# Column slabs as one 512-column product: both activation parts into two halves of a bank

## Chip, cores, metric

One core of a Trainium2 chip (trn2). The metric is the device time of one launch in microseconds; every run is timed alone.

## What is computed

The kernel computes a float32 forward pass over 256 tokens of width 1024: two layers (a gated recurrence with pooling, then a convolution block; each followed by cross-attention and a convolutional FFN), and a third layer with banded attention and a mixture of 32 experts. The part that the change touches most is the FFN, twice, with `D_FF = 3072` and `CONV_F = 3`:

```python
def conv_ffn(x, norm, w_up, dw_w, dw_b, w_down):
    h = rms_norm(x, norm) @ w_up
    g = causal_dwconv(h[..., :D_FF], dw_w, dw_b)
    u = h[..., D_FF:]
    return (jax.nn.gelu(g) * u) @ w_down
```

The other products that change are `k = m @ wk` and `q = rms_norm(x) @ wq` of the cross-attention, the pointwise product `h = rms_norm(x) @ w1 + b1; h = glu(h)` of the convolution block, and the first columns and the gates of the third layer's in-projection `x @ w_in`.

## The kernel before

**Layout.** Activations lie turned: 128 channels on the partitions, 256 tokens along the free side (`T = 256`), eight chunks for the width (`KC = 8`). Weights come from memory as *slabs* of 128 x 1024 floats through a ring of 12 places (`raw`), issued by SyncE in the order of `PHASES`. A *column slab* holds the weights of 128 output columns for all eight chunks; `col_slab` multiplies it and leaves 128 x 256 results in one of four PSUM banks `pw` (512 floats wide, used to the half). A *row slab* holds 128 input rows for all 1024 outputs and adds into the four banks `acc`.

**Split products.** Products must keep float32 accuracy, so each factor is held as a sum of a high and a low part in a shorter format (fp32r). ScalarE writes the high part of a slab (`wh`, line 733), VectorE (line 1259, every second slab) or POOL (line 1142, the others) subtracts to get the low part (`wl`). Both have four places (`SPLIT`), filled three slabs ahead (`AHEAD`). The activations are split likewise into `ah`, `al` (and `mh`, `ml` for the memory tokens). `tile3` (lines 2064 to 2066) makes the product of one chunk with three matmuls, high x high, low weight x high, high weight x low, all into the same 256 columns:

```python
pe.matmul(dst, wh[...], hi, start=start, stop=False)
pe.matmul(dst, wl[...], hi, start=False, stop=False)
pe.matmul(dst, wh[...], lo, start=False, stop=stop)
```

**Norms.** A product starts on the unnormed activation; the reciprocal root mean square of each token (`rstd_b`) is multiplied in when VectorE takes the result out of its bank. The first three slabs of a phase (`LEAD`, function `lead`) run ahead of that and stay with the three 256-column products; the taking out ("drain") of a slab is `col_out` (lines 1327, 1329), `slab_out` (1393, first keys), `gate_out` (1749, fills) and `gate` and `up` in the FFN (1570, 1589).

**The FFN loop** (`glu`, J = 24 steps, four of them in the body of a hardware loop). Step j on TensorE: gate slab j, up slab j, row slab j - 2. On VectorE: drain of the gate slab into `gpad` (with two zero columns ahead), three taps of the convolution (1576, then 1579 twice) into `cf`, drain of the up slab into `uf`, and `hid = cf * uf` (1592) once ScalarE has put the GELU on `cf`; its splits stand between. ScalarE and POOL then split `hid` for the row slab. A bank is free for TensorE when its drain has raised `empty_v` (`bank_free`); two steps use the four banks in turn.

**Order.** Every engine's order is written out by hand, and semaphores count it. `V.fence()` makes VectorE wait for its own last instruction. In the third layer's attention 16 gate columns ("fills", `FILLS`) run between the score products; all use bank `pw[3]`, so each waits for the drain of the one before (`gate_out`). After the in-projection the expert weights (1 MB per transfer) come through a ring of 18 places, and the last quarter of the run multiplies them as they land.

## Time and profile before

| | |
|---|---|
| median of 3 runs | 1674.98 us (1674.19 to 1675.51) |
| span of the profiled execution | 1674.9 us |
| TensorE busy (matmul) | 1628.1 us, 97% |
| TensorE weight loads | 1290.0 us, 77% |
| VectorE busy | 830.0 us, 50% |
| ScalarE, POOL busy | 601.2 us, 471.2 us |
| memory read, written | 394.02 MB, 1.05 MB |

The times are whole runs; the span is one profiled execution, from its first to its last instruction, and the profile gives no other time for it; it lies 0.1 us under the median. Busy time of TensorE is that of overlapping matmuls with modelled ends, so what a matmul costs is read from the distance between starts. Shares are means over stages with different limits; the stages are looked at one by one.

### The profile page before, as it was taken

The page shows a single profiled execution, that of the slowest core. Times are in us where ns is not written, and L with a number is a line of the kernel's source. Part 1 is how long each engine was busy: PE and PEld are TensorE (multiplying, and loading weights), DVE is VectorE, ACT ScalarE, POOL GpSimd, SP SyncE. Part 2 cuts the span into 40 slices and gives each one's busy share as a digit, 9 for nine tenths or more (in the row PEclk, how much of TensorE's full clock was granted, in tenths as well). Part 3 has the DMA queues.
Part 4 walks back from the last instruction along what each step waited for, and adds up shares of the span by engine and source line. Part 5 has one row for each costly group of instructions (what it writes and reads, how often), then busy time and mean ns, then how long its engine had stood idle before and what let it go on. Part 6 is the DMA issues. An engine that isn't in the chain of part 4 may idle for free.

```text
span 1674.9 us, 28612 instructions
## 1 busy us (share of the span) xinstructions
PE 1628.1 (97%) x11476; PEld 1290.0 (77%) x11476; DVE 830.0 (50%) x1320; ACT 601.2 (36%) x1019; POOL 471.2 (28%) x257
## 2 busy tenths in 40 slices
PE   7999999999999999999999999999999999999996
PEld 6898998999999699899999998888944444444332
DVE  2665457888875174688887433768711010110102
ACT  2371454444453264444345333656311111111101
POOL 1332424555543142355555443222200000000000
PEclk9999999999999999999999999999999999999999
DMA  7464634555559453455552665262899999999995
GB/s 296 151 218 157 211 114 139 184 180 176 182 183 262 165 165 116 136 188 176 179 185 90 209 217 176 89 229 87 319 394 421 421 422 421 421 422 420 421 421 220
DMA packets 86055, 401.21 MB, mean 240 GB/s; under 512 B 9536, under 2 KB 14272, under 8 KB 61248
## 3 DMA queue, kind: packets, MB, share of 16 engines
q1 hardware_dynamic: 84944, 395.81, 64.5%
q10 hardware_dynamic: 1008, 3.96, 0.6%
q8 instruction: 74, 1.21, 0.3%
q14 instruction: 29, 0.24, 0.0%
HBM read 394.02 MB, written 1.05 MB: 236 GB/s over the span
## 4 chain that ended last, share of the span: by engine, by line
PE 42%; issue 30%; DVE 22%; ACT 4%; POOL 1%; DVEq 1%; DMA 0%; ACTq 0%; SPq 0%; POOLq 0%
DVE wl L1259 6%; DVE cf L1576 5%; PE pw L2064 5%; PE pw L2066 5%; PE pw L2065 5%; PE pw L2377 4%; DVE hid L1592 4%; ACT wh L733 3%; DVE cf L1579 3%; PE acc L2070 2%; PE acc L2064 2%; PE acc L2065 2%; PE acc L2066 2%; PE acc L2236 2%; DVE gpad L1570 1%
## 5 line engine op out<-in xcount | busy, mean ns | idle before, releaser
L1142 POOL TENSOR_TENSOR wl<-raw,wh 128x1024 fp32r<-128x1024 f32 x157 | 387.4, 2468 | 569.4 <-ACT wh L733 565.7
L733 ACT ACTIVATE wh<-raw 128x1024 fp32r<-128x1024 f32 x314 | 325.1, 1051 | 230.8 <-PE pw L2066 104.9
L2064 PE MATMUL pw<-ah,wh 128*128 128x256 f32 x1272 | 364.5, 287 | 5.0 <-POOL wl L1142 3.4
L2065 PE MATMUL pw<-ah,wl 128*128 128x256 f32 x1272 | 359.8, 283 | 0.0
L2066 PE MATMUL pw<-al,wh 128*128 128x256 f32 x1272 | 359.8, 283 | 0.0
L1259 DVE TENSOR_TENSOR wl<-raw,wh 128x1024 fp32r<-128x1024 f32 x157 | 200.9, 1280 | 117.2 <-ACT wh L733 117.0
L2064 PEld LDWEIGHTS pw<-ah,wh 128*128 128x128 f32 x1272 | 243.7, 192 | 10.4 <-issue 6.3
L2065 PEld LDWEIGHTS pw<-ah,wl 128*128 128x128 f32 x1272 | 243.9, 192 | 0.1
L2066 PEld LDWEIGHTS pw<-al,wh 128*128 128x128 f32 x1272 | 243.8, 192 | 0.0
L2064 PE MATMUL acc<-yh,wh 128*128 128x256 f32 x672 | 194.0, 289 | 2.0 <-POOL yl L1211 1.2
L2065 PE MATMUL acc<-yh,wl 128*128 128x256 f32 x672 | 190.1, 283 | 0.0
L2066 PE MATMUL acc<-yl,wh 128*128 128x256 f32 x672 | 190.0, 283 | 0.0
L1153 POOL TENSOR_TENSOR small<-small 128x2 f32<-128x2 f32 x12 | 12.1, 1005 | 527.9 <-DVE small L1276 523.6
L2064 PEld LDWEIGHTS acc<-yh,wh 128*128 128x128 f32 x672 | 128.6, 191 | 5.7 <-issue 3.1
L2065 PEld LDWEIGHTS acc<-yh,wl 128*128 128x128 f32 x672 | 128.7, 192 | 0.1
L2066 PEld LDWEIGHTS acc<-yl,wh 128*128 128x128 f32 x672 | 128.7, 192 | 0.0
L2015 DVE COPY slot_gate<-pw 64x1 f32<-64x1 f32 x32 | 5.0, 156 | 235.0 <-ACT slots_to_tokens L1088 234.5
L1576 DVE TENSOR_SCALAR cf<-gpad,cols 128x256 f32<-128x256 f32 x48 | 90.2, 1879 | 7.5 <-DVE gpad L1570 6.9
L2377 PE MATMUL pw<-x_gained,raw 128*128 128x256 f32 x320 | 74.0, 393 | 8.3 <-DMA raw<-in_stream 8.3
L886 ACT ACTIVATE cf<-cf 128x256 f32<-128x256 f32 x48 | 20.1, 418 | 164.4 <-DVE cf L1579 164.1
L2656 PE MATMUL pw<-raw,gathered 128*64 128x512 f32 x328 | 77.0, 601 | 1.2 <-DMA raw<-in_experts 0.8
L1211 POOL TENSOR_TENSOR yl<-hid,yh 128x256 fp32r<-128x256 f32 x48 | 50.2, 1045 | 96.9 <-ACT yh L890 96.9
(335 smaller groups left out, 2569.2 us busy)
## 6 DMA issues: line engine op xcount, KB each, us to landing
raw<-in_stream SPq DMA_DIRECT2D x358, 512.0 KB, 3.5
raw<-in_experts SPq DMA_DIRECT2D x65, 1024.0 KB, 24.3
ring_w<-in_experts SPq DMA_DIRECT2D x40, 1024.0 KB, 24.3
ring_y<-in_experts SPq DMA_DIRECT2D x30, 1024.0 KB, 23.0
early_e<-in_experts SPq DMA_DIRECT2D x22, 1024.0 KB, 20.8
ring_q<-in_experts SPq DMA_DIRECT2D x11, 1024.0 KB, 21.9
ring_k<-in_experts SPq DMA_DIRECT2D x11, 1024.0 KB, 22.7
ring_a<-in_experts SPq DMA_DIRECT2D x11, 1024.0 KB, 23.4
```

Source lines behind the costliest of these rows:

```text
L733: A.done(act.activation(wh[:, s.base % SPLIT, :], raw[:, slot_of(s.base), :], ACT.Copy), w_hi)
L1142: G.done(pool.tensor_tensor(wl[:, s.base % SPLIT, :], raw[:, slot_of(s.base), :], wh[:, s.base % SPLIT, :].bitcast(F32), ALU.subtract), w_ ...
L1211: G.done(pool.tensor_tensor(yl[:, j % 4, :], hid[:, j % 2, :], yh[:, j % 4, :].bitcast(F32), ALU.subtract), S("ffn_hid_lo"))
L1259: V.done(dve.tensor_tensor(wl[:, s.base % SPLIT, :], raw[:, slot_of(s.base), :], wh[:, s.base % SPLIT, :].bitcast(F32), ALU.subtract), w_lo_v)
L1576: V.done(dve.tensor_scalar(cf[:, j % 2, :], gpad[:, j % 2, 2:T + 2], w, col(f"f_dw_b{l}", j, 4, i), ALU.mult, ALU.add))
L1579: V.done(dve.scalar_tensor_tensor(cf[:, j % 2, :], gpad[:, j % 2, 2 - k:T + 2 - k], w, cf[:, j % 2, :], ALU.mult, ALU.add), S("ffn_conv") ...
L1592: V.done(dve.tensor_tensor(hid[:, j % 2, :], cf[:, j % 2, :], uf[:, j % 2, :], ALU.mult), S("ffn_hidden"))
L2064: pe.matmul(dst, wh[:, s.base % SPLIT, w], hi, start=start, stop=False, **kw)
L2065: pe.matmul(dst, wl[:, s.base % SPLIT, w], hi, start=False, stop=False, **kw)
L2066: return pe.matmul(dst, wh[:, s.base % SPLIT, w], lo, start=False, stop=stop, **kw)
L2377: last = pe.matmul(pw[u % 4][:, 0:T], raw[:, slot_of(n), k * P:k * P + P], ax[:, k, :], start=(k == 0), stop=(k == KC - 1))
L2656: ins = pe.matmul(pw[bank + h][rows, :], stationary(e), expert_pair(s.base - S0["moe"])[:, e, 512 * h:512 * h + 512], start=first, stop=la ...
```

## The change

The high and the low part of an activation become one tile `a_pair` (and `m_pair`) with two halves. `tile2` replaces `tile3` in column slabs that are not of the first three: one matmul streams both halves past `wh` (512 columns, the whole bank: left half high x high, right half high weight x low), and one of 256 columns adds low weight x high to the left half. VectorE now has to add the two halves: `halves_added` with one reduction where nothing is multiplied (the keys), `halves_scaled` with two multiplications by `rstd_b` (the low half into a spare tile, the high half in place) and then an addition. In the FFN the sum stays in the bank, the convolution reads it there, and so does the product `hid`; `gpad` and `uf` go. A gate bank is then free when the last tap is done (`ffn_conv`), an up bank when `hid` is done (`ffn_hidden`), and `bank_free` waits for these.

```diff
+            def halves_added(bank, dst, sem):
+                V.done(dve.tensor_reduce(dst, bank[:, 0:2 * T].rearrange("p (h t) -> p t h", h=2), AX.X, ALU.add), sem)
+            def halves_scaled(bank, low, scale=None):
+                high = bank[:, 0:T]
+                V.fence()
+                for dst, src in ((low, bank[:, T:2 * T]), (high, high)):
+                    if scale is None:
+                        V.done(dve.tensor_tensor(dst, src, rstd_b[:], ALU.mult))
+                    else:
+                        V.done(dve.scalar_tensor_tensor(dst, src, scale, rstd_b[:], ALU.mult, ALU.mult))
+                V.fence()
+                return high
...
             def col_out(name, n, dst, scale=None, by=None, slab=None):
                 if by is None:
-                    ins = dve.tensor_copy(dst, b)
-                elif scale is None:
+                    halves_added(pw[u % 4], dst, empty_v)
+                    return
+                if name != "abin" and n >= LEAD:
+                    low = t[1][:] if name == "win" else low_t[:]
+                    ins = dve.tensor_tensor(dst, halves_scaled(pw[u % 4], low, scale), low, ALU.add)
+                    V.done(ins, empty_v)
+                    return
...
-                    V.done(dve.tensor_tensor(gpad[:, j % 2, 2:T + 2], pw[(USE0[name] + 2 * j) % 4][:, 0:T],
-                                             rstd_b[:], ALU.mult), empty_v)
+                    bank = pw[(USE0[name] + 2 * j) % 4]
+                    g = bank[:, 0:T]
+                    if 2 * j >= LEAD:
+                        halves_scaled(bank, low_t[:])
+                        V.done(dve.tensor_tensor(g, g, low_t[:], ALU.add))
+                    else:
+                        V.done(dve.tensor_tensor(g, g, rstd_b[:], ALU.mult))
...
-                            V.done(dve.tensor_scalar(cf[:, j % 2, :], gpad[:, j % 2, 2:T + 2], w,
-                                                     col(f"f_dw_b{l}", j, 4, i), ALU.mult, ALU.add))
+                            V.done(dve.tensor_scalar(cf[:, j % 2, :], g, w, col(f"f_dw_b{l}", j, 4, i),
+                                                     ALU.mult, ALU.add))
...
-                    V.done(dve.tensor_tensor(uf[:, j % 2, :], pw[u % 4][:, 0:T], rstd_b[:], ALU.mult), empty_v)
+                    up_b = pw[u % 4][:, 0:T]
+                    if 2 * j + 1 >= LEAD:
+                        halves_scaled(pw[u % 4], low_t[:])
+                        V.done(dve.tensor_tensor(up_b, up_b, low_t[:], ALU.add))
...
+                    V.done(dve.tensor_tensor(hid[:, j % 2, :], up_b, cf[:, j % 2, :], ALU.mult), S("ffn_hidden"))
...
-                    V.done(dve.tensor_tensor(gt[:, n - 46, :], pw[3][:, 0:T], rstd_b[:], ALU.mult), S("gate_out"))
+                    V.done(dve.tensor_tensor(gt[:, n - 46, :], halves_scaled(pw[3], t[1][:]), t[1][:], ALU.add), S("gate_out"))
...
+            def tile2(bank, s, n, pair, start, stop):
+                w = slice(n * P, n * P + P)
+                pe.matmul(bank[:, 0:2 * T], wh[:, s.base % SPLIT, w], pair, start=start, stop=False,
+                          skip_group_check=True)
+                return pe.matmul(bank[:, 0:T], wl[:, s.base % SPLIT, w], pair[:, 0, :], start=False, stop=stop,
+                                 skip_group_check=True)
...
-                    pe.wait_ge(empty_v, (jj + -2).of(lambda n: v0 + 2 * n + (1 if kind == "g" else 2)))
+                    pe.wait_ge(S("ffn_conv" if kind == "g" else "ffn_hidden"), (jj + -1).of(lambda n: n + ffn0(name)))
```

TensorE, the first two chunks of the first key slab (`pw` is the bank, `mh` and `ml` the parts of the memory tokens). Before:

```order
L2064 MATMUL pw<-mh,wh 128x256
L2065 MATMUL pw<-mh,wl 128x256
L2066 MATMUL pw<-ml,wh 128x256
L2064 MATMUL pw<-mh,wh 128x256
L2065 MATMUL pw<-mh,wl 128x256
L2066 MATMUL pw<-ml,wh 128x256
```

and with the change:

```order
L2100 MATMUL pw<-m_pair,wh 128x512
L2102 MATMUL pw<-m_pair,wl 128x256
L2100 MATMUL pw<-m_pair,wh 128x512
L2102 MATMUL pw<-m_pair,wl 128x256
```

Six matmuls for two chunks become four.

VectorE, the fourth step of the first FFN loop, ahead of the hardware loop (`wl` is a split of a later slab, `cf` the convolution, `pw` a bank). Before:

```order
L1570 TENSOR_TENSOR gpad<-pw,rstd_b 128x256
L1576 TENSOR_SCALAR cf<-gpad,cols 128x256
L1579 SCALAR_TENSOR_TENSOR cf<-gpad,cols,cf 128x256 x2
L1589 TENSOR_TENSOR uf<-pw,rstd_b 128x256
L1592 TENSOR_TENSOR hid<-cf,uf 128x256
L1259 TENSOR_TENSOR wl<-raw,wh 128x1024
```

and with the change:

```order
L1329 TENSOR_TENSOR low_t<-pw,rstd_b 128x256
L1329 TENSOR_TENSOR pw<-pw,rstd_b 128x256
L1596 TENSOR_TENSOR pw<-pw,low_t 128x256
L1603 TENSOR_SCALAR cf<-pw,cols 128x256
L1606 SCALAR_TENSOR_TENSOR cf<-pw,cols,cf 128x255
L1606 SCALAR_TENSOR_TENSOR cf<-pw,cols,cf 128x254
L1329 TENSOR_TENSOR low_t<-pw,rstd_b 128x256
L1329 TENSOR_TENSOR pw<-pw,rstd_b 128x256
L1619 TENSOR_TENSOR pw<-pw,low_t 128x256
L1624 TENSOR_TENSOR hid<-pw,cf 128x256
L1259 TENSOR_TENSOR wl<-raw,wh 128x1024
```

The two drains are now three instructions each, all on the bank, and the taps and `hid` read the bank; the split keeps its place at the end.

## Rows read from the trace of the kernel before

**Rows 1.** The page, busy time of each engine, share of the span and instructions.
```profile
PE 1628.1 (97%) x11476; PEld 1290.0 (77%) x11476; DVE 830.0 (50%) x1320; ACT 601.2 (36%) x1019; POOL 471.2 (28%) x257
```

**Rows 2.** The page, lines on the chain of work that ended last, shares of the span.
```profile
DVE wl L1259 6%; DVE cf L1576 5%; PE pw L2064 5%; PE pw L2066 5%; PE pw L2065 5%; PE pw L2377 4%; DVE hid L1592 4%; ACT wh L733 3%; DVE cf L1579 3%; PE acc L2070 2%; PE acc L2064 2%; PE acc L2065 2%; PE acc L2066 2%; PE acc L2236 2%; DVE gpad L1570 1%
```

**Rows 3.** Table by stretch: us; busy of PE, PEld, DVE, ACT, POOL; PEclk, DMA share, GB/s.
```profile
275.45:465.34 189.89, 189.28 (x1561) 188.04 (x1561) 156.11 (x168) 81.01 (x113) 103.86 (x55) 1.00 0.55 180
1041.00:1122.00 81.00, 78.39 (x663) 67.61 (x660) 55.17 (x96) 48.35 (x109) 18.51 (x8) 1.00 0.38 132
1230.00:1640.00 410.00, 402.23 (x2028) 167.53 (x2028) 38.99 (x88) 56.64 (x102) 0.00 (x0) 1.00 1.01 419
```

**Rows 4.** TensorE in time, FFN loop: start, length, engine, line, operation (x count) [idle].
```profile
400.05 0.28 PE L2066 MATMUL pw<-al,wh 128*128 128x256 f32 x1
...
400.17 0.28 PE L2064 MATMUL pw<-ah,wh 128*128 128x256 f32 x1
```

**Rows 5.** TensorE in time, value slabs of the in-projection.
```profile
1010.04 0.39 PE L2200 MATMUL pw<-wh,al 128*128 128x512 f32 x1
1010.26 0.39 PE L2198 MATMUL pw<-wh,ah 128*128 128x512 f32 x1
```

**Rows 6.** VectorE in time, two steps of the FFN loop.
```profile
400.02 0.42 DVE L1589 TENSOR_TENSOR uf<-pw,rstd_b 128x256 f32<-128x256 f32 x1
400.57 2.44 DVE L1592 TENSOR_TENSOR hid<-cf,uf 128x256 f32<-128x256 f32 x1
404.44 1.23 DVE L1259 TENSOR_TENSOR wl<-raw,wh 128x1024 fp32r<-128x1024 f32 x1 [1.44 <-ACT wh L733]
...
406.32 1.75 DVE L1576 TENSOR_SCALAR cf<-gpad,cols 128x256 f32<-128x256 f32 x1 [0.19 <-DVE gpad L1570]
408.22 1.11 DVE L1579 SCALAR_TENSOR_TENSOR cf<-gpad,cols,cf 128x256 f32<-128x256 f32 x2
...
412.64 2.46 DVE L1576 TENSOR_SCALAR cf<-gpad,cols 128x256 f32<-128x256 f32 x1 [0.19 <-DVE gpad L1570]
...
417.53 0.42 DVE L1589 TENSOR_TENSOR uf<-pw,rstd_b 128x256 f32<-128x256 f32 x1
```

**Rows 7.** POOL in time, the same stretch.
```profile
400.33 2.40 POOL L1142 TENSOR_TENSOR wl<-raw,wh 128x1024 fp32r<-128x1024 f32 x1 [2.89 <-ACT wh L733]
...
412.55 2.40 POOL L1142 TENSOR_TENSOR wl<-raw,wh 128x1024 fp32r<-128x1024 f32 x1
```

**Rows 8.** Instructions on tile gpad: ns min/median/max, first and last start.
```profile
L1570 DVE TENSOR_TENSOR gpad<-pw,rstd_b x48: 424/425/427, 264.0 to 890.6; 128x256 f32<-128x256 f32 x48
```

**Rows 9.** VectorE in time, queries of layer 0.
```profile
196.07 1.09 DVE L1329 SCALAR_TENSOR_TENSOR q_t<-pw,rstd_b 128x256 f32<-128x256 f32 x3
```

**Rows 10.** VectorE by line and shape: busy us, mean ns | idle before, releaser.
```profile
L1576 DVE TENSOR_SCALAR cf<-gpad,cols 128x256 f32<-128x256 f32 x48 | 90.2, 1879 | 7.5 <-DVE gpad L1570 6.9
...
L1779 DVE TENSOR_REDUCE small<-sc 128x2 f32<-128x514 f32 x8 | 5.5, 688 | 0.3
...
L1447 DVE TENSOR_SCALAR z<-pw,cols 128x256 f32<-128x256 f32 x4 | 2.2, 540 | 3.0 <-PE pw L2070 3.0
```

**Rows 11.** Waits of TensorE, start of FFN 0: us in total, times, longest.
```profile
PE pw L2064 <- POOL wl L1142: 1.7, 1, 1.7
```

**Rows 12.** VectorE in time, start of FFN 0.
```profile
267.46 0.85 DVE L1576 TENSOR_SCALAR cf<-gpad,cols 128x256 f32<-128x256 f32 x1
```

**Rows 13.** VectorE in time, queries of layer 0, slabs 5 and 7.
```profile
204.33 0.42 DVE L1329 SCALAR_TENSOR_TENSOR q_t<-pw,rstd_b 128x256 f32<-128x256 f32 x1 [1.34 <-PE pw L2066]
...
212.54 0.42 DVE L1329 SCALAR_TENSOR_TENSOR q_t<-pw,rstd_b 128x256 f32<-128x256 f32 x1 [1.43 <-PE pw L2066]
```

**Rows 14.** VectorE in time, pointwise product of the convolution block.
```profile
504.70 2.20 DVE L1645 TENSOR_SCALAR t<-t 128x256 f32<-128x256 f32 x1 [0.99 <-ACT t L919]
```

**Rows 15.** TensorE in time, second fill product in attention.
```profile
1048.89 0.35 PE L2064 MATMUL pw<-ah,wh 128*128 128x256 f32 x1 [0.61 <-DVE gt L1749]
```

**Rows 16.** The chain in order of time, first in-projection on unsplit data.
```profile
42.01 44.90 PE pw L2377 x208
```

More of the change, by code:

```diff
@@ L361, in program @@
         cv = sb("cv", "arena", 34, [P, KC, T])
-        gpad = sb("gpad", "arena", 24, [P, 2, T + 2])
         cf = sb("cf", "arena", 27, [P, 2, T])
-        uf = sb("uf", "arena", 29, [P, 2, T])
         hid = sb("hid", "arena", 31, [P, 2, T])
+        low_t = sb("low_t", "arena", 33, [P, T])
         q2 = sb("q2", "arena", 0, [P, 20, T])
@@ L1588, in up @@
                     V.fence()
-                    V.done(dve.tensor_tensor(uf[:, j % 2, :], pw[u % 4][:, 0:T], rstd_b[:], ALU.mult), empty_v)
+                    up_b = pw[u % 4][:, 0:T]
+                    if 2 * j + 1 >= LEAD:
+                        halves_scaled(pw[u % 4], low_t[:])
+                        V.done(dve.tensor_tensor(up_b, up_b, low_t[:], ALU.add))
+                    else:
+                        V.done(dve.tensor_tensor(up_b, up_b, rstd_b[:], ALU.mult))
                     V.fence()
                     dve.wait_ge(S("ffn_act"), (jj + 1).of(lambda n: n + ffn0(name)))
-                    V.done(dve.tensor_tensor(hid[:, j % 2, :], cf[:, j % 2, :], uf[:, j % 2, :], ALU.mult),
-                           S("ffn_hidden"))
-                V.fence()
-                V.done(dve.memset(gpad[:, :, 0:2], 0.0))
+                    V.done(dve.tensor_tensor(hid[:, j % 2, :], up_b, cf[:, j % 2, :], ALU.mult), S("ffn_hidden"))
                 trips, rest = glu_steps(J)
@@ L2095, in drain, with col_slab @@
             def drain(u):
-                for who, sem in (("v", empty_v), ("a", empty_a)):
+                for who, sem in emptier.items():
                     if u and emptied(u - 1, who):
                         pe.wait_ge(sem, emptied(u - 1, who))
-            def col_slab(s, u, hi, lo, wait_n=None, first_ready=None):
+            def col_slab(s, u, pair, wait_n=None, first_ready=None):
                 wait_split(pe, s)
@@ L2108, in col_slab, with col_phase @@
                         first_ready(k)
-                    last = tile3(pw[u % 4][:, 0:T], s, k, hi[:, k, :], lo[:, k, :], k == 0, k == KC - 1)
+                    last = tile2(pw[u % 4], s, k, pair[:, :, k, :], k == 0, k == KC - 1)
                 last.then_inc(slab_done, 1)
-            def col_phase(name, n, hi, lo, ready=None, hook=None, straight=None, s_off=0, u_off=0):
+            def col_phase(name, n, pair, ready=None, hook=None, straight=None, s_off=0, u_off=0):
                 s0, u0 = S0[name] + s_off, USE0[name] + u_off
@@ L2119, in col_phase @@
                         wait_emptied(pe, u0 + k - 4)
-                    col_slab(At(s0 + k), u0 + k, hi, lo, None, ready if k == 0 else None)
+                    col_slab(At(s0 + k), u0 + k, pair, None, ready if k == 0 else None)
                     if hook:
@@ L2125, in col_phase @@
                         for j in range(straight, straight + 4):
-                            col_slab(At(s0 + j, 4, i), u0 + j, hi, lo, i * 4 + (v0 + j - 3))
+                            col_slab(At(s0 + j, 4, i), u0 + j, pair, i * 4 + (v0 + j - 3))
             def lead(phase, name, pair):
@@ L2449, in final_spread @@
                     norm_spread("final")
-            col_phase("win", 32 - LEAD, ah, al, spread_at("mix"), final_spread, 5, LEAD, LEAD)
+            col_phase("win", 32 - LEAD, a_pair, spread_at("mix"), final_spread, 5, LEAD, LEAD)
             for b in range(3):
@@ L2478, in fill @@
                         for k in range(KC):
-                            last = tile3(pw[3][:, 0:T], s, k, ah[:, k, :], al[:, k, :], k == 0, k == KC - 1)
+                            last = tile2(pw[3], s, k, a_pair[:, :, k, :], k == 0, k == KC - 1)
                         last.then_inc(slab_done, 1)
```

43 lines of the change are left out of this document (22 added, 21 removed).

## Prediction

> **What bounds the kernel now.** I read the page's busy shares first [rows 1]: TensorE is busy in 97% of the span. That share is an average, so the chain of waits comes next [rows 2]: three of the costliest lines on it are VectorE's, the split (line 1259), the first convolution op of the FFN (line 1576) and the last product there (line 1592). So somewhere VectorE sets the pace under a TensorE that looks full. The table by stretch [rows 3] says where to look: the first FFN loop takes 189.89 us with TensorE busy all the time; the attention stage with its fill products has 2.6 us of idle TensorE in 81; the expert stage moves 419 GB/s with the DMA engines full, so it ends a fixed time after it can start, and what is won ahead of it is taken over whole.
>
> TensorE's price is read from starts, since the shown durations overlap. Products of 256 columns follow each other every 0.12 us [rows 4], those of 512 columns every 0.227 [rows 5]. At 2.4 GHz (granted clock 1.00 in all three stretches) the columns alone are 0.107 and 0.213, so both carry the same 0.013. The loop has 65 slabs of 24 products: 65 x 2.88 = 187.2 of its 189.89 us. The other 2.7 us are VectorE's: from one `uf` at 400.02 to the one two steps on at 417.53 are 17.51 us [rows 6], where six slabs want 17.28. In these two steps `hid` takes 2.44 and `cf` 1.75 and 2.46; each ends where a POOL subtraction ends (400.33 + 2.40, 412.55 + 2.40) [rows 7]. VectorE ops with both tensor inputs in SBUF wait for POOL there; `gpad`, with an input in PSUM, took 424 to 427 ns in all 48 cases [rows 8].
>
> **The product.** 175 slabs change: 8 (first keys), 2 x 5 (queries), 2 x 45 (FFN), 13 + 8 (pointwise, second keys), 46 (in-projection with its fills). Three products per chunk at 3 x 0.12 become one of 512 and one of 256: 0.227 + 0.12 = 0.347. A slab falls from 2.88 to 8 x 0.347 = 2.776, by 0.104; 18.2 us if TensorE set the pace everywhere. The two extremes: nothing saved (the third part's 256 columns cost in the long product what they cost alone: 0), or the short product also loses its fixed part, its weights loaded behind a long one (0.335 a chunk, 0.2 a slab). I take the rows as they stand.
>
> **VectorE's new work.** A drain was one op; now it is low half times scale, high half times scale in place, and the add. Prices: back to back 0.34 (three `q_t` in 1.09) [rows 9]; behind a fence 0.55 (`uf` to `hid` 0.55) to 0.61 (0.42 and a gap of 0.19) [rows 6]. So a drain costs some 0.9 more. Writing to PSUM stands in no row: below, 0.42 as for SBUF; above, twice that. I take 0.42, the figure for the same op with the same input, and keep the other as a rival.
>
> **The FFN loops.** A gate becomes 0.34 + 0.55 + 0.61, then the convolution from the bank: 0.54 by the nearest op with two column operands and a PSUM input [rows 10] and 0.15 of fence, two taps 1.19 with theirs (1.11 for the pair) [rows 6]; 3.4 together. The up half is 0.34 + 0.55 + 0.55 + 0.46 = 1.9. Two steps with three splits at 1.26: 2 x 5.3 + 3.8 = 14.3 us, since `cf` and `hid` now have only one input in SBUF and should not wait for POOL. The VectorE page of the Trainium skill (VectorE: DVE Perf Modes, "Rules for kernel authors") advises to copy a product to SBUF first if many ops read it, as this kernel does now. By that advice the old convolution would be the better one; here it meets POOL in most steps and takes 1.88 us in the mean [rows 10], so I follow the rows.
> TensorE then needs 4 x 2.776 + 2 x 2.88 = 16.86 for two steps, more than 14.3, and becomes the bound: 42 column slabs and 23 row slabs are 182.8 us against 189.89, so -7.1. The bank is now freed by the last tap and not the first drain, and the other by `hid`; each is used again two steps later, some 14 us after its slab, so that wait is covered by the loop itself. If the cover went, it would show as TensorE waiting at a gate slab. At the start of a loop TensorE stands 1.7 us for a POOL split [rows 11], at the end of a chain through gate and up of steps 0 and 1. There the up of step 1 gains 0.9 and a convolution op loses 0.3 (0.85 to 0.54) [rows 12]; +0.6, and the gain of the first slabs vanishes in that stall. Net -6.4 a loop, **-12.9** for both.
>
> **First keys.** Eight drains become a reduction over both halves: 0.69 for some 512 elements [rows 10] instead of 0.42. VectorE hands over the first values late already, so the slabs' 0.8 is not seen: **+0.5**.
> **Queries, twice.** The drain of slab 5 stands ahead of the first row maxima (204.33) and that of slab 7 ahead of the second (212.54) [rows 13]; TensorE waits for the exponentials behind them. Two longer drains less the shorter slabs: +1.2 each, **+2.4**.
> **Pointwise and second keys.** 21 slabs give -2.2. In a pair VectorE had 5.76 us with a wait of 0.99 for tanh and an op held for 2.20 [rows 14]; now 1.25 (split) + 2 x 1.4 + 0.99 + about 0.8 + 0.5 = 6.3 against 5.55. It falls behind 0.7 a pair, 4.6 in all; the split for three slabs ahead leaves about 3.3 of that unseen. The later key slabs catch up. **-0.9**.
> **In-projection.** 30 slabs in a row, VectorE needs 4.1 us of 5.55 for two: **-3.1**.
> **Fills.** 16 products share one bank, so the next one waits for the drain. Where it stands right behind it, as at 1048.89 (0.61 idle) [rows 15], the longer drain shows in full. I count four such at 0.75 and twelve at 0.2, which the score products cover mostly: 5.4, less 16 x 0.104: **+3.7**. Its ends: -1.7 (all covered) and +12 (all seen).
>
> SP, ACT and POOL get no instruction more or less. Sum: -12.9 + 0.5 + 2.4 - 0.9 - 3.1 + 3.7 = -10.3. The profiled span is 1674.9, the median of the runs 1674.98, so one correction serves both: **1664.5 us**. With each stage's ends it lies between 1656 and 1672.
>
> **Rivals.**
> A. *The product is not cheaper.* The 512-column product costs 0.24, as two of 256. For it: products on unsplit data of 256 columns and two passes follow every 216 ns (44.90 us for 208) [rows 16], which is the columns and nothing fixed. Against it: [rows 5], which are with split data. Then two FFN steps take 17.28, each loop wins 2.7 - 0.6 = 2.1, and the costs elsewhere stay (keys 0.5, queries 3.0 without the shorter slabs, fills 5.4): 1674.9 - 4.2 + 8.9 = 1679.6. The TensorE page of the Trainium skill (TensorE: Matmul & The Clock Gate, "Back-to-back issue gap") states columns over the clock plus 2.5 ns; by it a slab would win under 0.02 us and this rival would hold. The starts shown here carry 13 ns and disagree. It decides as soon as a slab wins less than about 0.03, where the other costs eat the gain.
> B. *VectorE stays the bound.* Writes to PSUM (eight in two steps) cost 0.85 instead of 0.42: 14.3 + 3.4 = 17.7 in two steps, 0.84 over TensorE's, 21 pairs: +17.6, and some 3 more in the other drains: 1685. For it: no row shows such a write. Against: reading PSUM cost nothing extra. It decides above 17.35 in two steps.
> C. *The short product gains too.* 0.335 a chunk, 2.68 a slab: two steps 16.5, each loop -10.5, the in-projection -6, the fills +2.2, the rest as above: 1652. For it: the products of [rows 16], which have no fixed part.
> D. *Attention pays more.* The fills cost +10 (for 3.7) and the queries +5 (for 2.4): 1673. For it: exactly these drains stand on a chain with exponentials; against: TensorE idles only 2.6 us there [rows 3], so most drains have cover.
> That the change does not do what it says is excluded: the matmul count of a slab falls from 24 to 16.
>
> **Numbers.** Forecast 0.60, A 0.08, B 0.06, C 0.11, D 0.15. Two runs of this kernel differ by 1.3 us at most; 0.2% is 3.3 us, about what can be told from no change. Faster (below 1671.6): forecast 0.60, C 0.11 and a third of D, 0.76. Same: the rest of D, 0.10. Slower: A and B, 0.14. The range goes from just under C to the middle between D and A: 1649 to 1678. It leaves out A, B and the far side of C.
>
> **What would show it.** Right: starts 0.227 and 0.12 apart in a column slab; the FFN loop at 183 us with 8.43 per step, `cf` near 0.55 and `hid` near 0.45 in every step; VectorE waiting for TensorE's slabs in it. Wrong: two steps still near 17.5 with VectorE on the chain (B), chunks at 0.36 (A), or TensorE waiting for the fills' drains for more than 10 us (D).

## The result and the profile after

The changed kernel takes 1681.3 us (median of 6, 1680.33 to 1683.36) against 1675.46 for the kernel before (median of 6): a ratio of 1.0038 (95% interval 1.0027 to 1.0048), 5.8 us slower where 10.5 us faster were forecast. In every later run the time stands 1.8 us above the span, so the profiled execution of before belonged to a launch of some 1676.7, 1.2 above its median; the two traces differ by 5.0. The span of a launch and its time, which the prediction set equal, are thus not the same. One of the eleven executions of run 3 below took 2293 us at a mean granted clock of 0.65; its median counts it, its ratio does not.

The page of the changed kernel, busy times and the lines on the chain:

```profile
PE 1614.7 (96%) x10076; PEld 1213.4 (72%) x10076; DVE 849.0 (51%) x1636; ACT 608.2 (36%) x1019; POOL 463.1 (28%) x257
...
PE pw L2100 16%; PE pw L2102 8%; PE acc L2093 4%; PE acc L2094 4%; PE acc L2095 4%; PE pw L2413 4%; PE acc L2107 2%; DVE wl L1259 2%; PE acc L2273 2%; PE pw L2186 1%; PE pw L2235 1%; PE pw L2237 1%; PE pw L2236 1%; PE pw L2187 1%; PE pw L2176 1%
```

TensorE has 1400 products less than in [rows 1] and is 13.4 us less busy, and VectorE's convolution and `hid` have left the chain of [rows 2]. The time won is idle time now. Where, the starts of TensorE's stages tell. In this table, worked out from the traces, the first row is the start of a stage in the kernel before (first product of it, us), the others how much later (+) the same start lies in another kernel; `run1` to `run11` are the experiments below:

```
          q0     wo0    FFN0   pw1    k1     conv   q1     FFN1   win    att    out    experts end
before    182.7  226.1  249.3  465.3  514.5  537.6  618.9  685.0  900.9  1039.7 1121.7 1216.9  1674.9
changed   +0.4   +1.1   +1.1   -3.4   +1.8   +3.2   +3.2   +3.6   -0.8   -2.7   +2.5   +3.8    +5.0
run1      +0.3   +1.0   +1.0   -3.5   +1.7   +2.7   +3.0   +3.4   -0.8   -2.8   +2.5   +2.4    +4.0
run2      -0.2   +0.5   +0.5   -3.8   -4.2   -4.6   -4.6   -4.2   -8.5   -11.8  -5.0   -5.1    -5.7
run3      +0.8   +1.5   +1.5   -2.8   -3.9   -4.3   -4.3   -3.9   -8.3   -10.2  -3.6   -3.7    -2.3
run4      +0.0   +0.7   +0.7   -3.7   +1.5   +2.5   +2.7   +3.2   -1.2   -3.1   -3.1   -3.3    -1.3
run5      +0.5   +1.3   +1.3   -3.2   -3.6   -4.0   -4.0   -3.5   -7.8   -9.9   -9.9   -10.0   -10.8
run6      -0.4   +0.3   +0.3   -5.9   -6.3   -7.0   -7.0   -6.3   -12.4  -14.9  -14.9  -15.0   -15.7
run7      -0.3   -0.3   -0.3   -3.0   -3.5   -3.5   -3.5   -3.5   -6.1   -6.6   -6.7   -6.8    -7.3
run8      +0.6   +1.3   +1.3   +8.7   +13.8  +14.9  +14.8  +15.3  +21.2  +19.7  +26.4  +26.3   +28.5
run9      -0.4   -0.4   -0.4   -6.5   -7.7   -8.4   -8.4   -8.5   -14.6  -16.7  -16.7  -16.9   -14.0
run10     +0.9   +1.6   +1.6   -2.7   +2.4   +3.5   +3.5   +3.9   -0.5   -3.8   +2.9   +4.2    +5.6
run11     -0.4   +0.3   +0.3   -4.0   +1.2   +2.2   +2.2   +2.7   -1.7   -3.6   +1.7   +1.6    +0.9
```

(`q0`, `q1` queries, `wo0` their output product, `pw1` pointwise, `k1` second keys, `conv` the convolution, `win` in-projection, `att` attention with its fills, `out` what follows them, `experts` the first expert product.) The changed kernel wins 4.5 and 4.4 us in the FFNs and 1.9 in the in-projection, and loses 6.6 between `pw1` and `conv`, 5.2 in attention and 2.5 behind it. The table by stretch for the FFN loop, the pointwise slabs with the second keys, and attention (us; busy of PE, PEld, DVE, ACT, POOL; PEclk, DMA share, GB/s), changed kernel:

```profile
275.45:461.90 186.45, 185.18 (x1228) 169.46 (x1228) 134.89 (x255) 85.19 (x115) 101.23 (x56) 1.00 0.56 184
461.90:540.80 78.90, 71.92 (x438) 61.52 (x436) 59.61 (x94) 28.80 (x43) 29.50 (x13) 1.00 0.64 184
1037.00:1124.20 87.20, 78.83 (x545) 60.88 (x545) 68.58 (x128) 48.31 (x109) 19.09 (x8) 1.00 0.33 122
```

and the second of these stretches in the kernel before:

```profile
465.30:537.60 72.30, 72.30 (x603) 70.79 (x602) 46.35 (x69) 30.27 (x43) 29.60 (x13) 1.00 0.80 215
```

Before, TensorE was never idle there; now it is for 7 of 78.9 us. The third row answers to the second of [rows 3]: 8.4 us idle where 2.6 were.

**The price of a chunk.** TensorE in time, changed kernel, FFN loop (the stretch of [rows 4]):

```profile
400.07 0.40 PE L2100 MATMUL pw<-a_pair,wh 128*128 128x512 f32 x1
400.31 0.28 PE L2102 MATMUL pw<-a_pair,wl 128*128 128x256 f32 x1
400.42 0.40 PE L2100 MATMUL pw<-a_pair,wh 128*128 128x512 f32 x1
400.65 0.28 PE L2102 MATMUL pw<-a_pair,wl 128*128 128x256 f32 x1
```

Over the loop the medians from start to start are 236 ns behind a long product and 117 behind a short one: 353 a chunk, 2.824 a slab. A slab wins 0.056 us, not 0.104.

**The FFN loop.** VectorE in time, changed kernel, part of one step (what answers to [rows 6]):

```profile
408.26 0.42 DVE L1329 TENSOR_TENSOR low_t<-pw,rstd_b 128x256 f32<-128x256 f32 x1 [1.80 <-PE pw L2102]
408.60 0.42 DVE L1329 TENSOR_TENSOR pw<-pw,rstd_b 128x256 f32<-128x256 f32 x1
409.06 0.43 DVE L1596 TENSOR_TENSOR pw<-pw,low_t 128x256 f32<-128x256 f32 x1
409.68 0.54 DVE L1603 TENSOR_SCALAR cf<-pw,cols 128x256 f32<-128x256 f32 x1 [0.19 <-DVE pw L1596]
410.37 1.11 DVE L1606 SCALAR_TENSOR_TENSOR cf<-pw,cols,cf 128x255 f32<-128x255 f32 x2
```

The convolution's first op takes 0.54 where it took 1.75 and 2.46, and VectorE waits 1.80 us for TensorE's slab: here TensorE has become the bound, as forecast.

**The pointwise slabs.** VectorE in time, changed kernel, one pair and the start of the next:

```profile
503.41 0.29 DVE L1674 TENSOR_SCALAR t<-t 128x256 f32<-128x256 f32 x1 [0.58 <-ACT t L919]
503.74 0.49 DVE L1676 SCALAR_TENSOR_TENSOR hpad<-t,cols,t 128x256 f32<-128x256 f32 x1
504.36 0.42 DVE L1329 TENSOR_TENSOR low_t<-pw,rstd_b 128x256 f32<-128x256 f32 x1
504.70 0.42 DVE L1329 TENSOR_TENSOR pw<-pw,rstd_b 128x256 f32<-128x256 f32 x1
505.16 0.42 DVE L1345 TENSOR_TENSOR t<-pw,low_t 128x256 f32<-128x256 f32 x1
505.50 3.32 DVE L1259 TENSOR_TENSOR wl<-raw,wh 128x1024 fp32r<-128x1024 f32 x1
508.95 0.42 DVE L1329 TENSOR_TENSOR low_t<-pw,rstd_b 128x256 f32<-128x256 f32 x1
...
512.84 3.33 DVE L1259 TENSOR_TENSOR wl<-raw,wh 128x1024 fp32r<-128x1024 f32 x1
```

and POOL beside it:

```profile
505.35 2.37 POOL L1142 TENSOR_TENSOR wl<-raw,wh 128x1024 fp32r<-128x1024 f32 x1 [4.96 <-ACT wh L733]
512.69 2.39 POOL L1142 TENSOR_TENSOR wl<-raw,wh 128x1024 fp32r<-128x1024 f32 x1 [4.96 <-ACT wh L733]
```

The splits of one pair to the next in the kernel before, and POOL beside them:

```profile
502.03 1.22 DVE L1259 TENSOR_TENSOR wl<-raw,wh 128x1024 fp32r<-128x1024 f32 x1
...
507.79 1.22 DVE L1259 TENSOR_TENSOR wl<-raw,wh 128x1024 fp32r<-128x1024 f32 x1
```

```profile
504.35 2.40 POOL L1142 TENSOR_TENSOR wl<-raw,wh 128x1024 fp32r<-128x1024 f32 x1 [3.36 <-ACT wh L733]
```

There the split is over before POOL starts. With the change the split of 128x1024 takes 3.32 us where it takes 1.23 alone [rows 6]: POOL began its own subtraction 0.15 us earlier, and VectorE's ends 1.1 us after POOL's. This repeats in all six pairs from 483 us on: 7.34 us from split to split, against 5.76 before and the 5.65 that TensorE needs for two slabs. Between 470 and 550 us 8 of VectorE's 12 splits last over 2 us; before, one did. The ops that write in place in the bank take 0.42 each, as those to SBUF.

**The fills.** Waits of TensorE in attention, changed kernel, for the drain of a fill (us in total, times, longest), and the same waits in the kernel before:

```profile
PE pw L2100 <- DVE gt L1778: 6.9, 9, 1.9
```

```profile
PE pw L2064 <- DVE gt L1749: 1.5, 2, 0.9
```

**Behind the last expert** a branch of TensorE's program, which jumps over a path for overfull experts, took 3.55 us in the changed kernel and 0.36 before (duration in ns: least, median, largest; start):

```profile
L2830 PEldq COMPARE_BRANCH  x1: 3552/3552/3552, 1664.2 to 1664.2; - x1
```

```profile
L2794 PEldq COMPARE_BRANCH  x1: 363/363/363, 1661.4 to 1661.4; - x1
```

TensorE stands in it while the squares for the last norm are ready: from the start of the branch to the end are 15.7 us, 13.5 before. In the router, from `out` to `experts`, another 1.3 us are lost: the granted clock was 0.90 over that stretch for 1.00 before, with a fall to 1.2 GHz inside it. Run 1 has the same instructions there, no such fall and no loss (table), and runs 2, 3, 8 and 10 have one in attention instead, where they lose some 6.7 us for 5.2; so this part belongs to the execution and not to the change. The experts took 1.0 us less, and 2.2 + 1.3 - 1.0 is the 2.5.

### The profile page after: what moved, and what is told of

Read it like the earlier page. It is cut to its first block, busy times and chain, and to the rows that moved or that the text cites. A ratio compares the mean times of both kernels' runs of the same rounds, so it can differ in the third digit from the quotient of the medians.

```text
span 1679.9 us, 26261 instructions
## 1 busy us (share of the span) xinstructions
PE 1614.7 (96%) x10076; PEld 1213.4 (72%) x10076; DVE 849.0 (51%) x1636; ACT 608.2 (36%) x1019; POOL 463.1 (28%) x257
## 4 chain that ended last, share of the span: by engine, by line
PE 59%; issue 29%; DVE 9%; ACT 2%; POOL 1%; DMA 0%; DVEq 0%; SPq 0%; POOLq 0%; ACTq 0%
PE pw L2100 16%; PE pw L2102 8%; PE acc L2093 4%; PE acc L2094 4%; PE acc L2095 4%; PE pw L2413 4%; PE acc L2107 2%; DVE wl L1259 2%; PE acc L2273 2%; PE pw L2186 1%; PE pw L2235 1%; PE pw L2237 1%; PE pw L2236 1%; PE pw L2187 1%; PE pw L2176 1%
## 5 line engine op out<-in xcount | busy, mean ns | idle before, releaser
L2100 PE MATMUL pw<-a_pair,wh 128*128 128x512 f32 x1272 | 455.6, 400 | 16.7 <-DVE gt L1778 6.9
L733 ACT ACTIVATE wh<-raw 128x1024 fp32r<-128x1024 f32 x314 | 328.7, 1053 | 247.2 <-PE pw L2102 118.6
L2102 PE MATMUL pw<-a_pair,wl 128*128 128x256 f32 x1272 | 356.9, 281 | 0.0
L2100 PEld LDWEIGHTS pw<-a_pair,wh 128*128 128x128 f32 x1272 | 239.0, 188 | 77.9 <-issue 14.3
L1259 DVE TENSOR_TENSOR wl<-raw,wh 128x1024 fp32r<-128x1024 f32 x157 | 216.8, 1381 | 94.9 <-ACT wh L733 94.7
L2102 PEld LDWEIGHTS pw<-a_pair,wl 128*128 128x128 f32 x1272 | 240.3, 189 | 0.1
L2413 PEld LDWEIGHTS pw<-x_gained,raw 128*128 128x128 f32 x320 | 62.5, 197 | 17.9 <-issue 8.6
L2031 DVE TENSOR_TENSOR expert_out_lo<-pw,expert_out_hi 128x512 fp32r<-128x512 f32 x32 | 20.7, 687 | 108.3 <-ACT expert_out_hi L1077 108.3
L1329 DVE TENSOR_TENSOR low_t<-pw,rstd_b 128x256 f32<-128x256 f32 x103 | 43.8, 425 | 49.5 <-PE pw L2102 38.9
L1211 POOL TENSOR_TENSOR yl<-hid,yh 128x256 fp32r<-128x256 f32 x48 | 44.8, 933 | 77.4 <-ACT yh L890 77.4
```

The costliest lines, as they stand in the source:

```text
L733: A.done(act.activation(wh[:, s.base % SPLIT, :], raw[:, slot_of(s.base), :], ACT.Copy), w_hi)
L1211: G.done(pool.tensor_tensor(yl[:, j % 4, :], hid[:, j % 2, :], yh[:, j % 4, :].bitcast(F32), ALU.subtract), S("ffn_hid_lo"))
L1259: V.done(dve.tensor_tensor(wl[:, s.base % SPLIT, :], raw[:, slot_of(s.base), :], wh[:, s.base % SPLIT, :].bitcast(F32), ALU.subtract), w_lo_v)
L1329: V.done(dve.tensor_tensor(dst, src, rstd_b[:], ALU.mult))
L2100: pe.matmul(bank[:, 0:2 * T], wh[:, s.base % SPLIT, w], pair, start=start, stop=False, skip_group_check=True)
L2102: return pe.matmul(bank[:, 0:T], wl[:, s.base % SPLIT, w], pair[:, 0, :], start=False, stop=stop, skip_group_check=True)
```

## The experiments

Times are medians; the kernel before took 1675.5 to 1675.9 in these comparisons.

**Run 1, layout.** The tiles become `[P, KC, 2, T]`, so that the halves of a chunk lie side by side.

```diff
-        a_pair = sb("a_pair", "ah", 0, [P, 2, KC, T], F32R)
+        a_pair = sb("a_pair", "ah", 0, [P, KC, 2, T], F32R)
```

> Only the layout of the two activation tiles changes: the halves of one chunk lie side by side, so the 512-column product reads one run of 512 floats and not two of 256. Seen in the changed kernel: starts 236 ns after a 512-column product and 117 after a 256-column one, 353 a chunk, where the value slabs show 227 for 512 contiguous columns. Theory A (the jump between the halves costs the 9 ns): 227 + 120 a chunk, a slab falls by 0.05 us, 84 FFN slabs, 27 of the in-projection and 16 fills gain 5 to 6 us, 1675.5 to 1676. Theory B (the 9 ns belong to the alternation of long and short products): 236 and 117 stay, 1681.

1680.91 us, ratio 1.0035 (1.0022 to 1.0049); the medians are 236 and 117 ns again. The jump between the halves costs nothing: theory A falls.

**Run 2, three products in the pointwise slabs.**

```diff
-            col_phase("pw1", 16 - LEAD, a_pair, spread_at("c"), None, 5, LEAD, LEAD)
+            col_phase("pw1", 16 - LEAD, (ah, al), spread_at("c"), None, 5, LEAD, LEAD)
...
-                if name != "abin" and n >= LEAD:
+                if name not in ("abin", "pw1") and n >= LEAD:
```

> The 13 pointwise slabs alone go back to three 256-column products and a drain of one instruction; all else stays changed. Theory: the 6.9 us that the changed kernel loses between the first pointwise slab and the last slab of the second keys come from VectorE's longer drains in the pointwise pairs (7.34 us a pair for 5.76). Then the pair returns to 5.76 and the time to about 1674. Rival: they come from the keys behind, whose drain is a reduction now (0.69 for 0.42): then it stays at 1680 to 1681.

1671.03 us, 0.9974 (0.9965 to 0.9983). From `pw1` to `conv` it now wins 0.8 us where the changed kernel lost 6.6: 7.4, as expected. The time fell by 3 us more than that. The branch is part of it, 0.48 us here; in this trace the in-projection, too, wins 3.3 us for 1.9 (see run 6).

**Run 3, the split one place earlier.** The same instructions; VectorE's split of the pointwise loop moves ahead of the drain of the even slab.

```diff
-                split(At(S0["pw1"] + n + AHEAD))
+                if not 4 <= n <= 15:
+                    split(At(S0["pw1"] + n + AHEAD))
+                elif n % 2 == 0:
+                    split(At(S0["pw1"] + n + 1 + AHEAD))
```

> The change is kept whole; in the pointwise loop VectorE's split stands one place earlier, ahead of the drain of the even slab, so that it can be done before POOL starts its own subtraction. No instruction more or less. Theory H (the hold is the loss: the split takes 3.31 us in each pair since it starts 0.15 us behind POOL's): the split takes 1.2, a pair falls from 7.34 to 5.7, the time to 1674 to 1675. Rival O (VectorE simply has too many instructions in a pair, as the prediction's 6.3 us had it): the pair stays at 6.3 or more and the time at 1677 or above.

1674.37 us, 0.9985 (0.9976 to 0.9995). VectorE in time, run 3:

```profile
499.20 1.23 DVE L1259 TENSOR_TENSOR wl<-raw,wh 128x1024 fp32r<-128x1024 f32 x1
500.56 0.42 DVE L1329 TENSOR_TENSOR low_t<-pw,rstd_b 128x256 f32<-128x256 f32 x1
...
504.66 1.22 DVE L1259 TENSOR_TENSOR wl<-raw,wh 128x1024 fp32r<-128x1024 f32 x1
```

and POOL:

```profile
500.65 2.40 POOL L1142 TENSOR_TENSOR wl<-raw,wh 128x1024 fp32r<-128x1024 f32 x1 [3.24 <-ACT wh L733]
```

The split ends before POOL starts, the pair takes 5.46 us with all six drain instructions in it, and the stretch from `pw1` to `conv` wins 1.5 us. So it is not the number of instructions (rival O) but the hold: the same work in another order is 8 us shorter there.

**Run 4, three products in the fills** (line 2515 back to `tile3`, `gate_out` back to one multiplication by `rstd_b`).

> The 16 fills alone go back to three products and a drain of one instruction. From the last value slabs to the last fill the changed kernel loses 5.3 us against before. Theory (the longer drain of the one bank that all fills share is seen in full where the next fill waits): 5 to 5.5 us less, 1676. Rival (the loss is elsewhere in attention, in the row maxima and exponentials that stand behind the drains only by chance): less than 2 us, 1679.5 to 1681.

1675.13 us, 0.9997 (0.9987 to 1.0006). From `att` to `out` nothing is lost (-3.1 at both ends), for 5.2 before: the waits for the drain are 1.5 us in 2 again. The run puts back products and drain together, but the three products of a fill take longer than the two, so it is the drain of the shared bank that costs the 5.2.

**Run 5, both put back.**

> Pointwise slabs and fills both go back to three products and a drain of one instruction; first and second keys, queries, FFN and in-projection stay changed. If the two losses are independent, as the stage table has them, they add: 1671.0 (pointwise alone) less the 6.2 of the fills alone gives 1665. If the fills' gain depends on when attention starts against the weight stream, less comes off: 1668 or more.

1664.3 us, 0.9935 (0.9922 to 0.9949). The two losses add: the change without its two bad places is 11 us faster than the kernel before.

**Run 6, long products first**, on top of run 5.

```diff
+            def slab2(bank, s, pair, first_ready=None):
...
+                for k in range(KC):
...
+                    pe.matmul(bank[:, 0:2 * T], wh[:, s.base % SPLIT, k * P:k * P + P], pair(k), start=(k == 0), stop=False,
+                              skip_group_check=True)
+                for k in range(KC):
+                    last = pe.matmul(bank[:, 0:T], wl[:, s.base % SPLIT, k * P:k * P + P], pair(k)[:, 0, :], start=False,
+                                     stop=(k == KC - 1), skip_group_check=True)
```

> As the run with pointwise slabs and fills put back, but a slab makes its eight 512-column products first and its eight 256-column ones after them. Theory (the 6 ns by which a chunk is dearer than 227 + 120 belong to the change between long and short): starts 227 and 120 apart, a slab 2.78 for 2.82, 111 slabs with TensorE as the bound, 5 us below that run. Rival (they belong to the long product with these weights, or to nothing that the order changes): 353 a chunk as before, the same time within 1 us.

1662.56 us, 0.9922 (0.9908 to 0.9935). In the FFN the mean from start to start is 230.6 ns between long products, 226.7 from the last long to the first short and 118.9 between short ones: about 2.79 a slab for 2.82. The stages win 1.7 us in each FFN and 0.4 in the in-projection, some 4 in all. The two traces differ by 4.8 and the medians by 1.7: the profiled execution of run 5 lay 1.6 above the median of its five, that of run 6 1.5 below its own, so how much of the 4 a launch keeps is open.

The order thus takes away some two thirds of the excess over the forecast price. But the alternation alone does not set the 353. In the in-projection the same alternating products can also run at the forecast price: they do so in runs 2 and 10. The starts of two long products that lie 24 chunks apart, changed kernel:

```profile
939.83 0.40 PE L2100 MATMUL pw<-a_pair,wh 128*128 128x512 f32 x1
...
948.31 0.40 PE L2100 MATMUL pw<-a_pair,wh 128*128 128x512 f32 x1
```

and run 2:

```profile
939.84 0.39 PE L2100 MATMUL pw<-a_pair,wh 128*128 128x512 f32 x1
...
948.16 0.39 PE L2100 MATMUL pw<-a_pair,wh 128*128 128x512 f32 x1
```

That is 353 ns a chunk and 347. In the changed kernel every third chunk takes some 360 and the others 350; in run 2 they take 344 and 350, and the stage (`win` to `att`) wins 3.3 us, where the runs with the slower rhythm win 1.5 to 2.1. What brings a stream into one rhythm or the other is open, and so is why long products behind one another vary between 227 and 236.

**Run 7, the bank-reading convolution alone**, in the kernel before, all products three.

```diff
-                    V.done(dve.tensor_tensor(gpad[:, j % 2, 2:T + 2], pw[(USE0[name] + 2 * j) % 4][:, 0:T],
-                                             rstd_b[:], ALU.mult), empty_v)
+                    b = pw[(USE0[name] + 2 * j) % 4][:, 0:T]
+                    V.done(dve.tensor_tensor(b, b, rstd_b[:], ALU.mult))
...
-                            V.done(dve.tensor_scalar(cf[:, j % 2, :], gpad[:, j % 2, 2:T + 2], w,
+                            V.done(dve.tensor_scalar(cf[:, j % 2, :], b, w,
```

> The kernel before with one part of the change alone: the FFN convolution and hid read the bank (drain in place, one multiplication), all products stay three. Theory (the old convolution's waits for POOL set the FFN's pace): no cf or hid is held, two steps fall from 17.51 to TensorE's 17.28, some 2.5 us a loop, 1670.5. Rival (the FFN's gain in the changed kernel is the product's alone): 1675, with two steps at 17.5.

1669.31 us, 0.9959 (0.9945 to 0.9972). VectorE by line and shape, run 7 (busy us, mean ns; then idle before), and `hid` in the kernel before:

```profile
L1575 DVE TENSOR_SCALAR cf<-pw,cols 128x256 f32<-128x256 f32 x48 | 26.1, 544 | 7.5 <-DVE pw L1570 6.9
...
L1592 DVE TENSOR_TENSOR hid<-pw,cf 128x256 f32<-128x256 f32 x48 | 20.4, 425 | 3.1
```

```profile
L1592 DVE TENSOR_TENSOR hid<-cf,uf 128x256 f32<-128x256 f32 x48 | 67.8, 1412 | 4.0
```

`cf` falls from 1879 ns in the mean [rows 10] to 544, `hid` from 1412 to 425. A loop wins 2.6 to 2.7 us: 1.6 within it, at 0.24 per two steps as expected (the first steps ran at 17.28 before, too), and nearly all the rest at its end. From the start of the last row slabs to the next stage are 8.6 us for 9.6, likely since the chain through convolution and `hid` is shorter.

**Run 8, the old convolution in the changed kernel** (the sum of the halves goes to `gpad` and `uf`, which convolution and `hid` read).

> The changed kernel with the other part of the FFN change taken back: each drain still adds two halves, but the sum goes to the old tiles in SBUF, which convolution and hid read. Theory: cf and hid wait for POOL again, and the four drains of two steps cost 0.9 more each; VectorE, already the bound before at 17.51, needs 19 to 21 us for two steps, 16 to 38 us more a loop, 1715 to 1755. Rival (VectorE has room, the waits fit into its idle time of 27 percent): two steps stay near 17.06, 1681 to 1686.

1704.2 us, 1.0164 (1.0148 to 1.0179). The same two lines, run 8:

```profile
L1606 DVE TENSOR_SCALAR cf<-gpad,cols 128x256 f32<-128x256 f32 x48 | 58.0, 1209 | 7.4 <-DVE gpad L1599 6.8
...
L1627 DVE TENSOR_TENSOR hid<-cf,uf 128x256 f32<-128x256 f32 x48 | 45.6, 950 | 3.1
```

The holds are back, and the first FFN loses 7.4 us where the changed kernel wins 4.5; in all 23 us over the changed kernel. Less than I expected: two steps take 17.8 us, not 19, the held ops lost less than before (1209 for 1879), and VectorE's busy share from 290 to 455 us rose from 72% to 83%, so it still had idle time. The direction holds, the size was a miss.

**Run 9, together:** long products first, side by side, early split, fills and queries with three products.

> What the runs so far single out, together: eight long products ahead of eight short ones, three products for the fills and the queries, the pointwise slabs changed with VectorE's split one place earlier, and the two halves of a chunk side by side. From the grouped run's 1662.6: pointwise slabs some 0.7 us less (the stage table of the run with the early split against the one with three products), queries 0.7 a layer less if their drains are what the changed kernel loses there (then the stretch from the FFN's rows before them to the output rows comes back to the kernel before's length). Layout, read from the starts: theory A (two runs of 256 cost the long product something once it follows its like): 227 between long products for 230.6 in the grouped run, 2.8 us over 111 slabs, 1657.5 in all. Theory B (layout does nothing): 230.6 again, 1660.5.

1660.84 us, 0.9908 (0.9892 to 0.9925), the fastest median, though its interval overlaps that of run 6. FFN and in-projection run as in run 6, so layout does nothing here either (theory B). The queries lose nothing now in either layer (`q0` to `FFN0`, `q1` to `FFN1`), where run 6 loses 0.7 in each. Changed pointwise slabs with the early split win 1.9 us from `pw1` to `conv`, for 1.1 with three products in run 6.

**Run 10, TensorE's program moved** by one-column products ahead of its first wait, in the changed kernel.

```diff
             pe.wait_ge(S("ones"), 1)
+            for _ in range(72):
+                pe.matmul(acc[0][0:32, 0:1], ones[:, 0:32], ones[:, 0:1], start=True, stop=True)
```

> The changed kernel with 72 products of one column added on TensorE ahead of its first wait for data, where it stands idle for 8.2 us; they change nothing but the place of all later instructions in TensorE's program (72 is the number of products by which the pointwise slabs differ between the changed kernel and the run with three products in them). Seen so far: TensorE's branch over the dense path, just ahead of the last norm, took 3.5 to 4.0 us in all five runs with changed pointwise slabs at their place (the changed kernel, the side-by-side layout, the early split, the fills with three products, the old convolution), and 0.36 to 0.48 in the kernel before and in the other five. Theory (the branch's length depends on where its target lies in TensorE's program): the branch takes 0.36 to 0.5 us here, the tail is 1.9 us shorter and the time 1679 to 1679.5 in place of 1681.3. Rival (it depends on something else in the pointwise slabs, or on chance): the branch takes 3.5 us and the time is 1681.

1682.67 us, 1.0040 (1.0027 to 1.0054). The branch took 2.38 us: it moved with the program, but not to 0.36. The trace shows 144 products for the 72 written, so the move was twice what I wanted. Nor were they free: they last until 8.9 us, and TensorE's first product on data starts at 8.84 for 8.24 in the changed kernel, so up to 0.6 us is lost at the start; a fall of the granted clock in attention (0.91 from 1105 to 1125 us, 1.00 in the changed kernel) costs some 1.4 more. From the branch to the end the trace is shorter, 14.6 us for 15.7, by the 1.2 that the branch is shorter. The time of this run therefore says nothing against the theory, but the branch's 2.38 does not meet it.

**Run 11, half of it.**

> The changed kernel with 36 instead of 72 one-column products ahead of TensorE's first wait. In the run with 72 the trace shows 144 products and 144 weight loads: one written product of whole floats becomes two, so that run moved the later instructions by twice what was meant; its branch took 2.38 us, not 3.55 and not 0.36. With 36 they move by 72 products and their weight loads, which is the difference between the changed kernel and the run with three pointwise products. Theory (the branch's length depends on the place of its target): 0.36 to 0.5 us, the tail 1.9 us shorter, 1679 to 1679.5. Rival (place does not decide; the length varies by itself between 2.4 and 4.0 wherever the pointwise slabs are changed): 2.4 or more, and 1681 to 1682.

1679.7 us, 1.0023 (1.0014 to 1.0032). The branch, run 11:

```profile
L2832 PEldq COMPARE_BRANCH  x1: 359/359/359, 1662.8 to 1662.8; - x1
```

At the place of run 2 it takes about what it takes there (0.48). From the branch to the end are 13.1 us for 15.7, and the median falls by 1.6; the intervals of the two ratios (1.0014 to 1.0032 here, 1.0027 to 1.0048 for the changed kernel) overlap a little. So the place decides, as far as one trace for each place can show it: the same instructions 72 products further on brought the branch from 3.55 to 0.36.

## Why the prediction was wrong

Forecast and trace by stage, in us (trace: differences along the row "changed" of the table above):

```
stage                       forecast   trace
first keys                  +0.5       +0.4
queries, two layers         +2.4       +1.1
FFN, two loops              -12.9      -8.9
pointwise and second keys   -0.9       +6.6
in-projection               -3.1       -1.9
fills                       +3.7       +5.2
behind attention             0         +2.5
sum                         -10.3      +5.0
```

**The step that failed** is the pointwise pair: "now 1.25 (split) + 2 x 1.4 + 0.99 + about 0.8 + 0.5 = 6.3". It has half of the miss. The others were together too high: with the split at 1.22 the pair takes 5.46 (run 3), under TensorE's 5.65, and nothing would be lost. What failed is the 1.25. I read in [rows 14] that a held op took 2.20 there, and dropped the hold as if it belonged to that op. It belongs to the meeting of a POOL subtraction with a VectorE instruction whose tensors all lie in SBUF. Between 240 and 540 us of the kernel before, all 19 first taps `cf`, 12 `hid` and 7 `t` that began within a POOL subtraction took 1.38 us or more, for 0.29 to 0.42 alone; in the changed kernel the 9 splits that did took 1.92 to 3.33, and no instruction with 256 columns on a bank took over 0.55. The longer drains moved the meeting from a small op, which before cost nothing since VectorE had room, to the split, on which the next slab hangs, and locked it there: behind the tanh ScalarE writes the high parts of two slabs one after the other, VectorE meanwhile has two small ops and a drain to do, and comes to its split 0.15 us after POOL has begun, in pair after pair. Run 3 shows it: in the other order the split takes 1.22 and 8 us come back.

**The product** was right in kind and mis-sized: "0.227 + 0.12 = 0.347" was 0.353 where long and short alternate, in the FFN of every trace. 0.048 us a slab over 84 FFN slabs is 4.0, which is the whole miss of the FFN term (-12.9 to -8.9), and over 30 slabs 1.4 of the in-projection's (1.2). I took the price from a stream of long products alone [rows 5]; run 6 shows that the order counts, and the in-projection of runs 2 and 10, at 0.347 in the same order, that it is not the whole reason. Rival A (0.36 and no gain) was nearer than I gave it credit for, but did not hold. That the time came out near its 1679.6 is chance: A has no loss in the pointwise slabs and none behind the experts.

**The FFN's reason** held: VectorE was the bound, the convolution's waits for POOL made it so, and reading the bank ends them (runs 7 and 8). Run 7 wins 2.7 of the 4.4 us of a loop by this alone, so more than half of the FFN's gain is the bank and not the product. Two steps take 17.05, which is 4 x 2.824 + 2 x 2.88, and TensorE does not wait in the loop. A PSUM write in place costs 0.42, so rival B is out. The SBUF page of the Trainium skill (SBUF — State Buffer, "Who interferes with whom") says that VectorE and POOL share a pair of ports under an exclusive lock and that the order of issue decides who blocks: a VectorE instruction with two SBUF inputs contends with a POOL instruction that reads SBUF, and one with at most one SBUF input does not, outside the two-port performance modes. This case agrees: 3.32 us for the split (two inputs) behind POOL, and 0.42 to 0.54 for the drains, first taps and `hid` on a bank. The first taps `cf` of [rows 6] and `t` of [rows 14] have one tensor input, in SBUF, and were held all the same, so "both tensor inputs in SBUF", as the prediction has it, is too narrow; they could fall under the page's exception, but no run here shows the mode of an instruction.

**The fills** were under-counted: "four such at 0.75 and twelve at 0.2" was nine waits and 6.9 us in the trace, and the stage lost 5.2 for 3.7. The end of +12 that I kept was far, the mechanism right. **The queries** cost half of what I took.

**What no row told me:** the branch, 1.6 of the 5.8 us by the medians of run 11 (2.7 by its trace, from the branch on). The change takes products out of TensorE's program, so everything behind moves; that the program's length at one place can cost time at another was in none of the rivals. The row below is all that the DMA queues did during the 3.55 us of it (queue, packets, MB, share): one transfer of instructions of 16 KB.

```profile
q8 instruction: 1, 0.02, 2.0%
```

In the kernel before and in run 11 a transfer of that size lies 10 us ahead of the branch and none in it. The pattern holds in all thirteen traces: in the six with a long branch such a transfer begins between 0.1 us before the branch's start and 1.6 after it, and the branch ends 1.42 to 1.47 us after the transfer; in the seven with a short one none lies in it, and the last one before it was done over 8 us earlier. So the branch ends with this load; that it holds the place to which the branch jumps the traces do not say. The Trainium skill (Advanced Engine Details and Errata, "ISA Cache") states that instructions are held in lines of 16 KB, 256 instructions each. Run 11 moved the program by 72 products and their 72 weight loads, which by that page's figure is about half a line (an estimate), and run 10 by twice as much, a little over a whole one: the first brought the branch from 3.55 to 0.36, the second, back near where it was in its line, only to 2.38. That fits in kind, no more.

That the slower kernel has a faster twin (run 5, 11 us) means that the chances were wrong in one place: I had put the risk on the product and on attention, and none on a stage in which VectorE had 1 us of slack in 5.76 and a hold of 2.

## What to carry to other kernels

A hold by POOL doesn't go away when the instruction that it struck gets off the path: ask which instruction will be there next, and if it is one that TensorE waits for, order it so that it runs before POOL starts. A change that pays in a stage bound by TensorE can be paid for in one where an engine behind it has no room, so make it stage by stage: here the FFN slabs and the in-projection wanted the long product, and 16 gates that share one bank didn't. Take the price of a product from a stream with the same neighbours, and allow for two: the same stream ran at 347 and at 353 ns a chunk here.

## What the runs showed of the hardware that I had not expected

- A 512-column product between 256-column ones is followed 236 ns later in the median, in the in-projection of runs 2 and 10 after 232, and in a stream of its like after 227 to 231; the layout of its 512 columns (one run or two) changes nothing.
- One branch on TensorE took 0.36, 0.48, 2.38 or 3.5 to 4.0 us in kernels that differ there only in the place of the program; 36 idle products of one column at the start of the kernel removed 3.2 us of it. A long branch ends 1.42 to 1.47 us after a 16 KB transfer of instructions.
- A product of whole floats with one column appears twice in the trace for each one written (144 for 72).
- In the last 20 us the granted clock of run 9 is 0.68 in the mean with the branch short, and 0.90 in run 5; from the experts' start to the end run 9 takes 2.9 us more than the kernel before, 2.3 of them ahead of the branch. Over the same last 20 us the clock is 0.67 in the changed kernel, 0.80 before and 0.81 in run 11. What lowers it in run 9 stays open.
